# Seam of the odd layer and the final product: order of loads and of the split work

## What is computed

```python
proj = h @ od_w_in[i]
q, k, v, r, a_lr = split_cols(proj, [GLA_K_WIDTH, GLA_K_WIDTH, GLA_V_WIDTH, GLA_V_WIDTH, GLA_GATE_RANK])
c_out = gla_mixer(q, k, v, a_lr, gla_w_a2[i], gla_b_a[i], gla_norm[i]) * jax.nn.silu(r)
mix = c_out @ od_w_out[i]
x = x + mix.astype(x.dtype)
...
return rmsnorm(x, final_norm)
```

## Time and profile before

| | |
|---|---|
| time, median of 3 runs | 1771.84 us (1764.5 to 1773.58) |
| the profiled execution's own time | 1775.91 us |
| its span, first to last instruction | 1774.0 us |
| TensorE busy | 1673.1 us, 94% of the span |
| VectorE busy | 859.3 us, 48% |
| ScalarE busy | 623.7 us, 35% |
| GpSimd busy | 280.4 us, 16% |
| mean granted TensorE clock | 0.982 of full speed |

### The profile page before, as it was taken

How to read it: one execution, slowest core, us unless ns; L and a number is a source line. 1 busy time by engine, 2 the same in 40 slices (tenths; PEclk the granted TensorE clock), 3 DMA queues, 4 the chain that set the end, 5 groups by cost and what they waited for, 6 DMA issues and landing times.

```text
span 1774.0 us, 22631 instructions
## 1 busy us (share of the span) xinstructions
PE 1673.1 (94%) x7910; PEld 1346.8 (76%) x7910; DVE 859.3 (48%) x1695; ACT 623.7 (35%) x1567; POOL 280.4 (16%) x500
## 2 busy tenths in 40 slices
PE   3998888999999869999999999999999999979997
PEld 3776666777777658888867888888888888868886
DVE  4767543466667556453343233343434444344443
ACT  4622232467666544332253122222222332131111
POOL 1865000000000161110000022221222211000000
PEclk9999998999999979999999999999999999989999
DMA  8344444445454676322232333333333332184663
GB/s 218 119 136 150 118 131 123 139 147 152 138 153 138 194 206 204 105 96 95 74 106 101 116 109 113 103 113 110 107 119 105 114 103 86 66 256 148 197 193 107
DMA packets 271817, 235.50 MB, mean 133 GB/s; under 512 B 81657, under 2 KB 224825, under 8 KB 271705
## 3 DMA queue, kind: packets, MB, share of 16 engines
q1 hardware_dynamic: 260408, 232.94, 42.1%
q10 hardware_dynamic: 11296, 1.12, 0.5%
HBM read 140.09 MB, written 93.91 MB: 132 GB/s over the span
## 4 chain that ended last, share of the span: by engine, by line
PE 60%; DVE 1%; DMA 1%; SPq 1%; issue 1%; ACT 0%; POOLq 0%; POOL 0%; ACTq 0%; DVEq 0%
PE odd_bank L2127 29%; PE odd_bank L2282 10%; PE odd_bank L2171 9%; PE odd_bank L2152 2%; PE odd_bank L2229 2%; PE odd_bank L2226 1%; PE odd_bank L2227 1%; PE odd_bank L2208 1%; PE odd_bank L2196 1%; PE odd_bank L2185 1%; DVE glu_g_lo L1972 0%; PE odd_bank L2210 0%; PE odd_bank L2136 0%; PE odd_bank L2237 0%; PE odd_bank L2236 0%
## 5 line engine op out<-in xcount | busy, mean ns | idle before, releaser
L2127 PE MATMUL odd_bank<-ht_hi,odd_w_hi 128*128 128x512 f32 x768 | 319.9, 416 | 1.1 <-DVE odd_w_lo L1889 1.1
L2127 PE MATMUL odd_bank<-ht_lo,odd_w_hi 128*128 128x512 f32 x768 | 300.5, 391 | 0.0
L2127 PE MATMUL odd_bank<-ht_hi,odd_w_lo 128*128 128x512 f32 x768 | 299.0, 389 | 0.0
L1185 PE MATMUL ev_acc<-ht_hi,ev_w_hi 128*128 128x512 f32 x576 | 242.5, 421 | 1.5 <-DVE ht_lo L891 1.5
L1185 PE MATMUL ev_acc<-ht_hi,ev_w_lo 128*128 128x512 f32 x576 | 228.7, 397 | 0.0
L1185 PE MATMUL ev_acc<-ht_lo,ev_w_hi 128*128 128x512 f32 x576 | 228.3, 396 | 0.0
L1901 DVE COPY odd_stage<-odd_bank 128x512 f32<-128x512 f32 x96 | 66.4, 691 | 228.2 <-PE odd_bank L2127 228.2
L2127 PEld LDWEIGHTS odd_bank<-ht_hi,odd_w_hi 128*128 128x128 f32 x768 | 144.4, 188 | 40.3 <-issue 7.6
L2127 PEld LDWEIGHTS odd_bank<-ht_lo,odd_w_hi 128*128 128x128 f32 x768 | 144.1, 188 | 32.0
L2127 PEld LDWEIGHTS odd_bank<-ht_hi,odd_w_lo 128*128 128x128 f32 x768 | 144.7, 188 | 27.1
L1185 PEld LDWEIGHTS ev_acc<-ht_hi,ev_w_hi 128*128 128x128 f32 x576 | 110.3, 192 | 30.6 <-issue 4.5
(11 more groups left out here) (286 smaller groups left out, 2943.4 us busy)
## 6 DMA issues: line engine op xcount, KB each, us to landing
odd_gl_in<-scr_heads SPq DMA_DIRECT2D x32, 640.0 KB, 4.2
scr_heads<-odd_stage SPq DMA_DIRECT2D x64, 256.0 KB, 2.0
odd_w_raw<-od_w_in SPq DMA_DIRECT2D x48, 256.0 KB, 3.6
ev_w_raw<-ev_w_in SPq DMA_DIRECT2D x36, 256.0 KB, 4.6
ev_x_tile<-x SPq DMA_DIRECT2D x16, 512.0 KB, 3.8
ev_s_cos_sin<-scr_s_cos_sin SPq DMA_DIRECT2D x32, 256.0 KB
odd_xo_sum<-x SPq DMA_DIRECT2D x16, 512.0 KB, 4.3
scr_x<-odd_xo_sum SPq DMA_DIRECT2D x16, 512.0 KB, 2.8
```

Of the source, the lines that this page charges most:

```text
L1185: mm = pe.matmul(acc[n % 3][:], w[j][:, k, :], h[:, k, t], start=(k == 0 and r == 0), stop=(k == KT - 1 and r == 2))
L2127: mm = pe.matmul(acc[n % 4][:], w[j][:, k, :], h[:, k, t], start=(k == 0 and q == 0), stop=(k == KT - 1 and q == 2))
```

## The change

The change orders the work of the seam anew; no matmul, pass or transfer is added or left out, and no wait of TensorE changes. `load_mix` is taken apart into `load_on` (GLA output) and `load_sil` (gate).

- SyncE: `load_on` of tiles 0 and 1 goes to slot 91; `load_xf` of tiles 0 and 1 and the load of `fn` go to slot 95; in slot 96 the gate of tile 0 stands behind weight block 1, blocks 2 to 7 follow it directly, and the gate of tile 1 comes last.
- ScalarE: no weight block in slot 97; in slot 98 blocks 0, 1, 2, then the upper part of tile 0, then 3 and 4; in slot 99 blocks 5 and 6; in slot 100 block 7.
- VectorE: in slot 98 `gated(0)`, blocks 0, 1, 2, the lower part of tile 0, block 3; in slot 99 blocks 4 and 5 and only then the SiLU; in slot 100 blocks 6 and 7 and then the SiLU; `gated(1)` and the lower part of tile 1 come behind the slots.

```diff
+        WF_AT = {98: (0, 1, 2, 3, 4), 99: (5, 6), 100: (7,)}
+        WF_LOW_AT = {98: (0, 1, 2, 3), 99: (4, 5), 100: (6, 7)}
...
+                def load_sil(t):
+                    j = t % 2
+                    if t == 0:
                         for s in range(4):
                             sp.wait_ge(stored[s], 16 * 23)
...
+                    if n == 91:
+                        load_on(0)
+                        load_on(1)
+                    if n == 95:
+                        load_xf(0)
+                        load_xf(1)
+                        sp.dma_start(fn, prm["final_norm"].rearrange("(o d) -> o d", o=1).broadcast_to([P, D])).then_inc(fn_in, 16)
                     if n == 96:
                         sp.wait_ge(acc_full, 96)
                         for k in range(KT):
                             sp.dma_start(wf_raw[:, k], prm["od_w_out"][0][k * P:(k + 1) * P, :]).then_inc(wf_in[k], 16)
                             if k == 1:
-                                load_mix(0)
-                                load_xf(0)
-                            if k == 3:
-                                load_mix(1)
-                                load_xf(1)
-                sp.wait_ge(acc_free, n_acc)
-                sp.dma_start(fn, prm["final_norm"].rearrange("(o d) -> o d", o=1).broadcast_to([P, D])).then_inc(fn_in, 16)
+                                load_sil(0)
+                        load_sil(1)
...
-                    if n >= 97:
-                        for k in ((0, 1), (2, 3), (4, 5), ())[n - 97]:
-                            act.wait_ge(wf_in[k], 16)
...
-                split_mix(0)
-                for k in (6, 7):
...
+                    for k in WF_AT.get(n, ()):
+                        if k == 3:
+                            split_mix(0)
+                        act.wait_ge(wf_in[k], 16)
+                        s.activation(wf_hi[:, k], wf_raw[:, k], ACT.Copy, scale=wn[:, k:k + 1]).then_inc(wf_hi_done, 1)
                 split_mix(1)
...
-                    if n >= 1 and accs[n - 1][0] >= R0:
+                    if n >= 1 and accs[n - 1][0] >= R0 and n < 99:
                         silu(n - 1)
...
+                    if n == 98:
+                        gated(0)
+                    for k in WF_LOW_AT.get(n, ()):
+                        if k == 3:
+                            lower(0)
+                        dve.wait_ge(wf_hi_done, k + 1)
...
+                    if n >= 99:
+                        silu(n - 1)
```

More of the change, by code:

```diff
@@ L1492, in store_ot, with load_on @@
                                  ot[:, i % 2]).then_inc(gl_stored[i % 2], 16)
-                def load_mix(t):
+                def load_on(t):
                     j = t % 2
@@ L1498, in load_mix @@
                             sp.wait_ge(gl_stored[s], 16 * (GH * NBLK // 2))
+                    if t >= 2:
+                        sp.wait_ge(m_lo_done, t - 1)
+                    sp.dma_start(m_on[:, j], scr["cmix"].rearrange("k p t -> p k t")[:, :, t * P:(t + 1) * P]).then_inc(mix_in[j], 16)
+                def load_sil(t):
+                    j = t % 2
+                    if t == 0:
                         for s in range(4):
@@ L1503, in load_mix @@
                             sp.wait_ge(stored[s], 16 * 24)
[L1504 to L1508, removed]
+                    sp.dma_start(m_sil[:, j], scr["sil"].rearrange("k p t -> p k t")[:, :, t * P:(t + 1) * P]).then_inc(mix_in[j], 16)
+                def load_mix(t):
+                    load_on(t)
+                    load_sil(t)
                 def load_xf(t):
@@ L1833, in silu_tanh, with split_mix @@
                     s.activation(tanh[:], stage[:, n % 4], ACT.Tanh, scale=0.5).then_inc(tanh_done, 1)
+                def split_mix(t):
+                    act.wait_ge(mul_done, t + 1)
+                    if t >= 2:
+                        act.wait_ge(f_full, 2 * t - 2)
+                    s.copy(m_hi[t % 2][:], m_on[:, t % 2]).then_inc(m_hi_done, 1)
                 act.wait_ge(prm_in, 80)
@@ L1857, in _ @@
                         s.preload_act_table_set(EXP_TANH)
-                    if n >= 97:
-                        for k in ((0, 1), (2, 3), (4, 5), ())[n - 97]:
-                            act.wait_ge(wf_in[k], 16)
[L1861 to L1867, removed]
-                split_mix(0)
-                for k in (6, 7):
-                    act.wait_ge(wf_in[k], 16)
-                    s.activation(wf_hi[:, k], wf_raw[:, k], ACT.Copy, scale=wn[:, k:k + 1]).then_inc(wf_hi_done, 1)
+                    for k in WF_AT.get(n, ()):
[3 more added lines that the diff above has]
+                        s.activation(wf_hi[:, k], wf_raw[:, k], ACT.Copy, scale=wn[:, k:k + 1]).then_inc(wf_hi_done, 1)
                 split_mix(1)
@@ L2051, in _, with gated, lower @@
                 v.memset(w2[:], 0.0).then_inc(made, 1)
+                def gated(t):
+                    j = t % 2
+                    dve.wait_ge(mix_in[j], 32 * (t // 2 + 1))
+                    v.scalar_tensor_tensor(m_on[:, j], m_on[:, j], 0.5, m_sil[:, j], ALU.mult, ALU.mult).then_inc(mul_done, 1)
+                def lower(t):
+                    j = t % 2
+                    dve.wait_ge(m_hi_done, t + 1)
+                    v.tensor_tensor(m_lo[j][:], m_on[:, j], m_hi[j].ap().bitcast(F32), ALU.subtract).then_inc(m_lo_done, 1)
                 dve.wait_ge(prm_in, 80)
@@ L2078, in _ @@
                             gate_log(k)
[L2079 to L2095, removed]
-                gated(1)
[L2097 to L2101, removed]
+                    if n == 98:
[4 more added lines that the diff above has]
+                        dve.wait_ge(wf_hi_done, k + 1)
+                        v.scalar_tensor_tensor(wf_lo[:, k], wf_raw[:, k], wn[:, k:k + 1], wf_hi[:, k].bitcast(F32),
+                                               ALU.mult, ALU.subtract).then_inc(wf_ready, 1)
+                    if n >= 99:
+                        silu(n - 1)
+                gated(1)
                 lower(1)
```

## The result

| | before | with the change |
|---|---|---|
| time, median | 1771.88 us (4 runs, 1764.5 to 1773.58) | 1761.51 us (4 runs, 1759.15 to 1762.56) |
| ratio, 95% interval | | 0.9946 (0.9932 to 0.9961) |
| profiled execution, own time and span | 1775.91, 1774.0 us | 1759.15, 1757.2 us |
| mean granted TensorE clock | 0.982 | 0.987 |

The kernel is 10.4 us (0.54%) faster; the interval reaches from 0.39% to 0.68%. It was forecast at 1760.5, or 11.3 us less. One execution of the loads-only kernel further down took 2402 us at a mean clock of 0.658, against 0.984 to 0.988 in its nine others, and its row leaves that one out.

A forecast was written before the change was run, and what follows sets the result against it. The seam was taken as set by a weight block tile 0 needs last, with first-needed instructions behind it. Loss of 13.2 us falling to 1.9 gives 11.3 off 1771.84, so 1760.5 us; range 1753 to 1768.

The forecast's parts named there:

- What bound the seam: Between projection and final product: a late weight block's transfer holds instructions tile 0 needs first; at most 13.2 us to win.
- The sum: Seam loss of 13.2 us before and 1.9 after, so 11.3 us less, giving 1760.5 us; chance 0.74.
- The 0.5 and 1.2 us of the forecast: TensorE's two waits expected in tile 0, for weight blocks 6 and 7, each costing 0.1 us more.
- VectorE and ScalarE, step by step: Slots 98 to 100: start times worked out from recorded paces, VectorE's block 7 starting at 1582.8 and ending at 1584.1.
- Transfers: Slot 96 queue: 512 KB worth 1.4 us, gate of tile 0 landing at 1568.2, blocks 2 to 7 at 1569.1 to 1576.1.
- the early rows: Two residual rows and norm weight sent in slot 95, ahead of store and gate; 0.5 us added to the gate.
- this rival: In Transfers: by ring order, slot 95's three early transfers delay store and gate; 2.9 us lost, 8.4 left; no separate chance.
- Early loads: GLA output loads in slot 91, about 27 us before the weight, beside one 256 KB store per slot; costed at nothing.
- The rival of the clock: TensorE's clock falls in the two short waits of tile 0; 2.3 us lost, gain 9.0, 1762.8 us; chance 0.07.
- The other side: VectorE's gated(0) starting no sooner than 1580.3 gains nothing, each us beyond is lost; say 1783 us; chance 0.03.

The follow-up runs named there:

- loads-only: SyncE's new order of transfers put into the kernel before, ScalarE and VectorE lists left old: 1765.88 us (9 runs), ratio 0.9970, seam 20.80 us.
- engines only: Changed kernel with SyncE's block of the kernel before, so only ScalarE and VectorE lists are new: 1763.80 us (7 runs), ratio 0.9957, seam 18.31 us.
- late gate: Changed kernel with the gate of tile 0 issued behind weight block 5 instead of block 1: 1759.11 us (1 run), seam 19.22 us.
- Nothing early: Changed kernel with residual rows and norm weight behind the second gate, GLA output back ahead of its gate in slot 96: 1760.54 us, seam 12.85 us.
- tile behind the weights: Kernel with all weight blocks in slot 98, with tile 0's split moved behind block 7: 1761.47 us (1 run), seam 16.18 us.
- SiLU first: Changed kernel with the SiLU of accumulations 98 and 99 back ahead of the weight blocks: 1761.75 us (1 run), seam 13.76 us.
- rows late: Changed kernel with the two residual rows and norm weight issued behind the second gate in slot 96: 1763.33 us (1 run), seam 12.85 us.

## Why the prediction was right

**What bound the seam.** Right. The instructions that tile 0 needs first stood behind those that it needs last. Loads only and engines only show that both lists took part, the engines' list with the larger share.

**The sum.** Forecast 11.3 us, measured 11.5 in the seam and 10.4 between the medians, inside the interval of 6.9 to 12.0 us (0.39% to 0.68% of 1771.88). The loss left was put at 1.9 and is 12.85 - 11.1 = 1.7: two waits of 0.30 and 0.87 recorded (0.46 and 1.03 by the starts), plus the two restarts of 0.1. The 0.5 and 1.2 us of the forecast stood at the blocks named. The medians bear the 11.5 out only within that interval, and the 16.8 us between the two profiled executions owe 5.3 to the part ahead of the seam, not to the change.

**VectorE and ScalarE, step by step.** The lists ran to a few tenths as worked out: block 7 starts 5.26 us after the last projection matmul where 5.4 was forecast, and the two idle times of 0.55 us ahead of blocks 5 and 7 are the waits for ScalarE that the working implied. This is what paces taken from rows can do where an engine's list is fixed and no transfer is late.

**Transfers.** The mechanism was right and the sizes were off, which the sum did not feel because the gate had margin either way. The gate was put 0.8 us ahead of its use and came 1.7 ahead. The GLA output that left the queue ahead of it was put at 1.4 us and measured 2.0; the 0.5 us charged for the early rows measured 0.4. The prediction's count of six other transfers among the weight blocks before is right; the seven told with the change are one too many, as the norm weight stood behind the blocks. The Trainium skill (DMA: Bandwidth & Descriptors, section "Queues, rings and completion order") gave this rival its ground, descriptors taken in ring order. By that rule the rows could hold up little more than the store, since all three had landed by 1554.5 (the norm weight 5.7 us after its issue at 1548.82) and the gate went out at 1555.72. The late gate agrees with the rule: with four weight blocks more in front of it the gate took 10.3 us from issue to landing instead of 6.3. Its whole delay was 6.0 us (4.26 past the use plus the 1.7 of margin); the other 2.0 came from its later issue.

**Early loads.** The forecast cost them at nothing, and by its own numbers they gained almost nothing: with the GLA output still ahead the gate would land at 1569.1 (1568.2 + 1.4 - 0.5), 0.1 us past its use. It did not draw that conclusion. Nothing early has the same seam.

**The rival of the clock.** Given 7 in 100, and it did not occur with the change; but the reason against it was too weak. The forecast set a single wait of 1.14 us that kept the clock against a standstill of 5 us that lost it, and left the range between them empty. The trace it was read from could have narrowed that range: early in the program, on smaller matmuls, the clock fell inside a wait of 2.96 us.

```profile
153.62 1.04 PE L1212 MATMUL ev_bank<-ev_s_cpow,ev_s_bbar 128*16 128x128 f32 x4 [2.96 <-DVE ev_s_cpow L1006]
```

```profile
152.00:153.00 1.00, 0.00 (x0) 0.00 (x0) 0.96 (x2) 0.00 (x0) 0.92 (x2) 0.87 0.00 0
```

Three experiments lie in the range and lost the clock: waits of 1.83 and 0.59 us (engines only), 0.87 and 1.43 us behind an earlier 1.51 (late gate), a single one of 3.13 us (tile behind the weights). Two seams kept it: 1.85 and 0.23 us (SiLU first), 0.30 and 0.87 us (the change). A single wait of 2.51 us, early in the trace of the late-gate kernel, kept it too:

```profile
650.61 0.50 PE L2158 MATMUL odd_bank<-glu_g_hi,ht_hi 128*128 128x512 f32 x1 [2.51 <-DVE glu_g_lo L1979]
```

```profile
651.00:653.00 2.00, 2.00 (x10) 1.64 (x9) 2.00 (x3) 1.55 (x2) 2.00 (x2) 1.00 0.86 234
```

So the change stands nearer to losing the clock than the forecast took it to; how near, no run measures. The Trainium skill (TensorE: Matmul & The Clock Gate, section "A second HAM failure mode: psum-queue depth-cycling") says that short idle stretches between groups of matmuls, where they come often enough, make the clock swing. The traces of engines only and late gate agree so far as the clock fell after short waits, once in each seam; the change and SiLU first, with two short waits each, kept it at 1.00. One row was too little to set this rival aside.

**The other side.** A late gate is charged one to one, as this rival said, and with the clock's 2.1 us on top. The point from which nothing is gained would thus come sooner than the 11.3 us past the use that was given; no run went that far.

## What to carry to other kernels

At a seam between two products, list what the first matmuls of the second one wait for, in the order in which they ask for it, and put transfers and passes into that order: whole operands before the pieces that a loop asks for one by one, and copies that nobody waits for behind both. An in-order engine makes one late operand the price of everything behind it, so look for the instruction that waits for another engine in the middle of a list: moving two copies with their tanh and SiLU behind the last weight block took the rest of the loss away. Loading earlier is worth nothing once a transfer beats its use; a margin is worth having where the next wait would also cost TensorE its clock.

## What was not expected of the hardware

- TensorE's granted clock fell to its lower level after waits that were each shorter than 2 us where two or three came close together (engines only, late gate), and after one of 3.13 us about 1.2 us into the resumed work (tile behind the weights: 0.94 in the microsecond from 1575, 0.50 in the next). The price was 1.4 to 2.3 us a time in these seams. The trace of the kernel before already showed a late fall: after a wait of 3.83 us that ended at 192.71, the granted clock was 0.85 in the microsecond from 193 and 0.50 in the next.
- The early part of the program, which no edit touched, varied by several us between profiled executions: the last projection matmul started at 1577.42 before, at 1572.15 with the change, and between 1565.71 (late gate) and 1576.32 (rows late) in the experiments. That is as much as the change gives, and why the seam had to be read by itself.
